# Two blocks in float32 on one core: in the last mixer the norms, the mask casts and the third output pair change place, and so does the preparation of x in the embedding before it

## The reference

```python
h = h + (p[i] @ ple_w_proj[i]) * sigmoid(rms_norm_2(h, ln_ple[i]) @ ple_w_gate[i])      # embedding
kv = rms_norm_2(h, kv_norm) @ w_kv            # k: rms_norm_2 over each head of 128, v plain
q = rms_norm_2(rms_norm_2(h, ln_mix[1]) @ w_q, q_norm) * 128 ** -0.5
# per head: A[t,s] = sigmoid(z_ts) * prod_{s<j<t} (1 - sigmoid(z_tj)), s < t;  o = A @ v
h = h + concat(o) @ w_out                     # then norm and the FFN
```

## Time and profile before

| | |
|---|---|
| median of 3 runs | 2504.65 us (2503.08 to 2505.79) |
| profiled execution | 2505.2 us |
| its span, first to last instruction | 2503.4 us |
| TensorE busy, of the span | 98% |
| VectorE, ACT, POOL busy | 68%, 50%, 54% |
| mean granted clock of TensorE | 0.996 |

### The profile page before, as it was taken

One profiled execution on the slowest core, in us unless ns is written; L12 is line 12 of the kernel. 1 busy time (PEld: TensorE's weight loads), 2 busy tenths in 40 slices (PEclk: granted clock), 3 DMA queues, 4 the chain that ended last, 5 costly groups with the idle time before them and its releaser, 6 DMA issues.

```text
span 2503.4 us, 37950 instructions
## 1 busy us (share of the span) xinstructions
PE 2456.0 (98%) x15202; PEld 2109.7 (84%) x15202; DVE 1710.7 (68%) x2551; ACT 1250.7 (50%) x1799; POOL 1358.0 (54%) x672
## 2 busy tenths in 40 slices
PE   9999999999999999999999999999999999999999
PEld 6899987777789999867878789999877777999987
DVE  6777752878587777586666677776587566777764
ACT  5434343568554333567555653333455685333343
POOL 4677744222457777346544357777444224777754
PEclk9999999999999999999999999999999999999999
DMA  4333333121323333222111123333332113233333
GB/s 142 101 102 101 102 122 107 58 68 51 91 95 102 102 102 102 85 85 85 51 35 35 51 93 102 102 102 110 94 95 83 49 34 101 102 102 101 102 104 124
DMA packets 61790, 223.64 MB, mean 89 GB/s; under 512 B 6704, under 2 KB 6832, under 8 KB 61488
## 3 DMA queue, kind: packets, MB, share of 16 engines
q1 hardware_dynamic: 60928, 218.07, 26.9%
q10 hardware_dynamic: 688, 3.15, 0.4%
HBM read 219.10 MB, written 2.10 MB: 88 GB/s over the span
## 4 chain that ended last, share of the span: by engine, by line
PE 80%; DVE 10%; ACT 6%; issue 3%; POOL 1%; DMA 1%; SPq 0%; DVEq 0%; ACTq 0%; POOLq 0%
PE ps L693 6%; PE ps L694 6%; PE ps L695 6%; PE ps L615 5%; PE ps L617 5%; PE ps L616 5%; PE ps L607 4%; PE ps L606 4%; PE ps L605 4%; PE ps L1045 2%; PE ps L1047 2%; PE ps L1046 2%; PE ps L667 2%; PE ps L1846 2%; PE ps L668 2%
## 5 line engine op out<-in xcount | busy, mean ns | idle before, releaser
L3015 POOL TENSOR_TENSOR w_lo<-raw,w_hi 128x1024 fp32r<-128x1024 f32 (+1 forms) x405 | 942.4, 2337 | 955.0 <-ACT w_hi L496 954.8
L496 ACT ACTIVATE w_hi<-raw 128x1024 fp32r<-128x1024 f32 (+1 forms) x405 | 396.8, 983 | 642.7 <-PE ps L607 392.5
L3022 POOL TENSOR_TENSOR t_lo<-t_sum,t_hi 128x1024 fp32r<-128x1024 f32 x140 | 336.2, 2423 | 60.0 <-DVE t_sum L805 36.5
L693 PE MATMUL ps<-mid_hi,w_hi 128*128 128x512 f32 x704 | 275.9, 392 | 3.4 <-DVE h L928 3.4
L694 PE MATMUL ps<-mid_lo,w_hi 128*128 128x512 f32 x704 | 275.6, 392 | 0.0
L695 PE MATMUL ps<-mid_hi,w_lo 128*128 128x512 f32 x704 | 274.8, 390 | 0.0
L615 PE MATMUL ps<-sx_hi,t_hi 128*128 128x256 f32 x840 | 238.4, 284 | 3.5 <-DVE ff_up L869 3.2
L616 PE MATMUL ps<-sx_lo,t_hi 128*128 128x256 f32 x840 | 237.7, 283 | 0.0
L617 PE MATMUL ps<-sx_hi,t_lo 128*128 128x256 f32 x840 | 237.7, 283 | 0.0
L928 DVE SCALAR_TENSOR_TENSOR h<-ps,h 128x512 f32<-128x512 f32 x320 | 200.4, 684 | 30.7 <-PE ps L695 20.5
L501 ACT ACTIVATE t_hi<-t_sum 128x1024 fp32r<-128x1024 f32 x140 | 147.3, 1060 | 103.6 <-DVE t_sum L803 65.8
(11 more groups left out here) (455 smaller groups left out, 6434.4 us busy)
## 6 DMA issues: line engine op xcount, KB each, us to landing
raw<-in_units_dram SPq DMA_DIRECT2D x406, 512.0 KB, 3.5
h<-in_x_t_dram SPq DMA_DIRECT2D x4, 512.0 KB, 7.7
toep<-in_rel_table_dram ACTq DMA_DIRECT2D x1, 2048.0 KB, 8.0
out_dram<-h SPq DMA_DIRECT2D x4, 512.0 KB, 5.5
p_f<-in_p_t_dram ACTq DMA_DIRECT2D x2, 512.0 KB, 3.7
const<-in_constants_dram SPq DMA_DIRECT2D x1, 832.0 KB, 8.2
vec<-in_vectors_dram SPq DMA_DIRECT2D x1, 137.5 KB, 2.0
```

What stands on the lines that cost most here:

```text
L496: nc.scalar.activation(w_hi[:, n % W_SLOTS, begin:], raw[:, n % RAW_SLOTS, begin:], ACT.Copy).then_inc(s_whi, 1)
L693: nc.tensor.matmul(out, hi, mid_hi[:, mid, :], start=(k == 0), stop=False)
L3015: nc.gpsimd.tensor_tensor(w_lo[:, n % W_SLOTS, begin:], raw[:, n % RAW_SLOTS, begin:], w_hi[:, n % W_SLOTS, begin:].bitcast(F32), ALU.subt ...
L3022: nc.gpsimd.tensor_tensor(t_lo[x % 2][part][:, :, :], t_sum[x % 2][part][:, :, :], t_hi[x % 2][:, 2 * part:2 * part + 2, :].bitcast(F32), ...
```

## The change

In `act_embed` and `dve_embed` the preparation of tile u-1 (its high half and square on ACT, its low half on VectorE) stands ahead of the sigmoid of step u and of the product behind it; VectorE's sum of squares stays behind the addition. In the mixer ACT's `norms` run behind that step's rounding and square. VectorE casts the masks ahead of the v columns. Half of the third pair's first unit (tiles 0 and 1, banks 1 and 2) runs after the values of head 6, half of its second unit (banks 6 and 7) between the suffixes and values of head 7, the two other halves behind the last head; both units count as used at the end. No instruction is added or removed.

```diff
@@ act_embed
                 if u:
                     act_ahead(act, n0, 0, u)
+                if gain is not None and u:
+                    act_prep(act, w, [u - 1], gain, lambda m: act.wait_ge(s_hup, w.hups + m + 1), x_hi=mid_hi)
                 act.wait_ge(s_free, b0 + u + 5)
                 nc.scalar.activation(ff_gate[:, u % 2, :], ff_gate[:, u % 2, :], ACT.Sigmoid).then_inc(s_gact, 1)
-                if gain is not None:
-                    if u:
-                        act_prep(act, w, [u - 1], gain, lambda m: act.wait_ge(s_hup, w.hups + m + 1), x_hi=mid_hi)
@@ dve_embed
                 nc.vector.tensor_tensor(ff_gate[:, u % 2, :], ps[:, 4 * g + u % 4, :], rstd[:, :], ALU.mult).then_inc(s_free, 1)
+                if gain is not None and u:
+                    dve_rest(dve, w, u - 1, gain, x_hi=mid_hi, x_lo=mid_lo)
                 dve.wait_ge(s_gact, (w.plo // 2 - 1) * 8 + u + 1)
...
                 if gain is not None and u:
-                    dve_prep(dve, w, [u - 1], gain, x_hi=mid_hi, x_lo=mid_lo)
+                    dve_square_sum(dve, w, u - 1, gain)
@@ pe_mixer3
-            def out_unit(unit, side, kp, final):
+            def out_unit(unit, side, kp, final, ms=range(4), done=1):
...
-                for m, bank in enumerate(SIDES3[side]):
+                for m in ms:
+                    bank = SIDES3[side][m]
...
-                        if m == 0:
+                        if m == ms[0]:
...
-                last.then_inc(s_used, 1)
-
-            out_unit(n_t, 0, 2, False)
-            out_unit(n_t + 1, 1, 2, False)
+                if done:
+                    last.then_inc(s_used, done)
...
             for x in range(8):
                 suffixes(x)
                 spare(STEP3[x][0])
+                if x == 7:
+                    assert next(stream, None) is None
+                    out_unit(n_t + 1, 1, 2, False, (2, 3), 0)
                 values(x)
                 spare(STEP3[x][1])
                 if x < 6:
                     scores(x + 2)
+                if x == 6:
+                    out_unit(n_t, 0, 2, False, (0, 1), 0)
                 spare(STEP3[x][2])
+            out_unit(n_t + 1, 1, 2, False, (0, 1), 0)
+            out_unit(n_t, 0, 2, False, (2, 3), 2)
             out_unit(n_t + 2, 0, 3, True)
             out_unit(n_t + 3, 1, 3, True)
@@ act_mixer3
             for u in range(16):
-                if u in (6, 10, 14):
-                    norms(u // 4 - 1)
                 if u:
                     act_ahead(act, n0, 0, u)
                     square(u - 1)
+                if u in (6, 10, 14):
+                    norms(u // 4 - 1)
@@ dve_mixer3
             layer = w.square_layer(4)
+            nc.vector.tensor_copy(tri_r[:, 0, :], mask["neg_tri"]).then_inc(s_tri, 1)
+            nc.vector.tensor_copy(tri_r[:, 1, :], mask["neg_ones"]).then_inc(s_tri, 1)
             dve.wait_ge(s_rcol, 2)
...
-            nc.vector.tensor_copy(tri_r[:, 0, :], mask["neg_tri"]).then_inc(s_tri, 1)
-            nc.vector.tensor_copy(tri_r[:, 1, :], mask["neg_ones"]).then_inc(s_tri, 1)
```

More of the change, by code:

```diff
@@ L2716, in spare @@
                     next(stream)
[L2718 to L2729, removed]
             w.unit += 8
@@ L2754, in out_unit @@
                         last.then_inc(s_bank, 1)
-                last.then_inc(s_used, 1)
-            out_unit(n_t, 0, 2, False)
-            out_unit(n_t + 1, 1, 2, False)
+                if done:
+                    last.then_inc(s_used, done)
+            for x in range(2):
+                scores(x)
+                spare(FIRST3[x])
+            for x in range(8):
+                suffixes(x)
+                spare(STEP3[x][0])
+                if x == 7:
+                    assert next(stream, None) is None
+                    out_unit(n_t + 1, 1, 2, False, (2, 3), 0)
+                values(x)
+                spare(STEP3[x][1])
+                if x < 6:
+                    scores(x + 2)
+                if x == 6:
+                    out_unit(n_t, 0, 2, False, (0, 1), 0)
+                spare(STEP3[x][2])
+            out_unit(n_t + 1, 1, 2, False, (0, 1), 0)
+            out_unit(n_t, 0, 2, False, (2, 3), 2)
             out_unit(n_t + 2, 0, 3, True)
```

## The result

The changed kernel takes 2510.95 us (median of 7 runs, 2510.27 to 2512.41), the kernel before beside it 2503.81 (2501.77 to 2505.79): ratio 1.0029, 95% interval 1.0020 to 1.0039, so slower by 5 to 10 us. The profiled execution took 2511.39 us, its span 2509.6, against 2503.4.

The account below looks back on a forecast made before the run. TensorE, busy 98% of the span, was taken to bound the kernel. Terms -2.8 - 0.9 + 0.5 + 2.3 + 2.2 + 4.4 = +5.7 us on 2505.2 gave 2510.9, or 2510.4 on the median's scale; range 2504.5 to 2515.

Parts of the forecast that it names:

- Norms, -2.8: Mixer steps 6, 10 and 14: norms behind the square spare TensorE 0.93 us three times; -2.8 us, bounds -2.8 to -2.0.
- Masks, -0.9: First head: TensorE waits for the third v column instead of the mask casts; -0.93 us, at most 1.3 gained.
- Embedding, +0.5: Embedding steps: POOL blocks VectorE's sum of squares each time, so TensorE's last k comes later; +0.5 us, bounds -1.5 to +1.5.
- Pair, +2.3: Around the last heads: the moved third pair waits 6.0 us for w_lo; net +2.3 us, bounds 2.0 and 2.8.
- Clock, +2.2: TensorE's clock falls to its lower level around the 6.0 us wait for w_lo; +2.2 us, bounds 1.7 and 3.4.
- FFN entry, +4.4: FFN's first gate unit: late roundings and blocked VectorE delay tile 7's low half; +4.4 us, bounds 2.5 and 6.
- rival 3: The clock falls once more, in the wait for x at the FFN; 1 to 2.5 us, total 2512.5; chance 0.20.
- in several pieces: Sign at the FFN's first unit: x_lo waited for by 3 us and more, split over several waits.
- Rival 1: FFN entry catches up: VectorE's first low half slips between POOL's two w_lo; x late 1 to 2, total 2507 to 2508; chance 0.21.
- Rival 2: Embedding gains what is meant: POOL falls on VectorE's gate, 1.5 us of lateness goes; total 2508.4; chance 0.10.
- Rival 4: Third pair finds its weights in time, so no long wait, low clock or late FFN entry; -6.9, 2497.7; chance 0.05.

Follow-up runs that it names:

- x first: The changed kernel with ScalarE's rounding of the third unit's weights and its successor at the FFN's entry behind preparing tiles 0 to 3: 2509.99 us, 1.0022.
- the best version: Kernel before plus norms, masks and pair moves, last-mixer weight rounding one unit earlier, FFN-entry roundings behind tiles 0 to 3; embedding as before: 2499.12 us, 0.9976.
- the rounding in head 1: The 2499.12 us kernel with ScalarE's extra weight rounding in head 1 instead of a second one in head 3: 2505.80 us, ratio 1.0002.

## Why the prediction was right, and where it was off

The forecast, 2510.4 and slower by over 0.2% most likely, came out (2510.95), and so did its main mechanism: the moved pair waits for a w_lo that ACT's order makes late, and the clock and the FFN's entry follow. That it came within 0.6 us is partly luck, as is told behind the terms. By its own steps, from the stages:

- **Norms, -2.8**: -2.8 in the run without the pair. In the changed kernel B to C is only 2.1 shorter, for a low-clock stretch (1846.2 to 1849.6) that falls into it. Ln and the next sum in its bank did not meet: no wait of L2592 is left here, not even that at the third unit, which comes right behind that stretch (0.4 without the pair).
- **Masks, -0.9**: -0.84; v in their place, as said.
- **Embedding, +0.5**: +0.55 to +0.65 without the clock. The blocked sum and the gate of step 7 are in the trace where the working put them. The sum takes 2.89, where the one behind it takes 0.69, and ends 0.55 after w_lo. The gate starts at 1840.81, which is 1841.96 on the scale of before (1.15 later), against 1842.0 by count. The exclusive lock of VectorE and GpSimd that the prediction took from the Trainium skill (SBUF — State Buffer, "Who interferes with whom") is borne out again here.

```profile
1838.00 2.89 DVE L551 TENSOR_TENSOR sum_sq<-sum_sq,sq 128x512 f32<-128x512 f32 x1
1840.81 0.68 DVE L2518 TENSOR_TENSOR ff_gate<-ps,rstd 128x512 f32<-128x512 f32 x1
...
1837.66 2.68 POOL L3021 TENSOR_TENSOR w_lo<-raw,w_hi 128x1024 fp32r<-128x1024 f32 x1 [2.84 <-ACT w_hi L496]
...
1845.21 0.50 PE L2607 MATMUL ps<-mid_hi,w_hi 128*128 128x512 f32 x1 [1.79 <-DVE mid_lo L540]
```

- **Missed, the clock at the mixer's start**: the two waits of before, 0.66 and 0.30 idle, became one of 1.79, and the clock fell behind it, worth about 0.9 (A to C lost 1.47 beside the norms' 2.8, and 0.54 in the run where the clock held). It fell in five of the six traces with the embedding's change, and in none of the seven without it. No term of the sum had it.
- **Pair, +2.3**: 2.3, once the matmuls in the wait keep the clock up. The wait is 5.92 past the pace against 6.0 by count. (The prediction's own steps, 2083.7 less 2081.3, give 2.4.)
- **Clock, +2.2**: 1.3. The low stretch began before the wait ended and covered only seven matmuls; 6.8 us of it cost 1.6 in the run with the pair alone and 1.4 in the one with x first. The mid value between two far rows was too high; the lower bound, 1.7, from the wait of the same kind, was the nearer.
- **FFN entry, +4.4**: 6.0. The count ends at the last x_lo, and that part held: it ends at 2102.99, 21.4 after the last pair's start (2081.63), against 20.9 by count and 16.5 before, so 4.9 later. The rest, about 1.1, is the clock, which fell in the wait. At half pace TensorE comes to the last tile at 2104.27, 1.3 after its x_lo was there; in the kernel before it began that tile 0.05 after. This is rival 3, to which the prediction gave 0.20 and 1 to 2.5 us. From the last pair's start to the end of the first unit it took 23.5, against 22 by count.
- **The wait there was of another kind.** The prediction had TensorE wait for x_lo "in several pieces". It waited once, ahead of the unit's first matmul, for VectorE to take h's tile 4 out of PSUM, and then found every x_lo ready when it came to it at half pace. No term or rival had this wait. The count still came near, because the same chain of VectorE makes both late. With x first on ScalarE the clock held and the pieces showed.
- **Rival 1** fell: VectorE's first low half began 0.57 behind the second w_lo, by the count's own margin. Its price was wrong too: in the run with the unused matmuls that low half did slip in first, and the stage was 1.3 longer all the same, with the next operation held by POOL instead. **Rival 2** fell in every run with the embedding's change. **Rival 4** needed a w_lo that starts before 2056.5; it started at 2058.54, which is 2061.9 on the scale of before (3.33 later at D).

The total fits better than the terms, and that is luck. The measured stages give +7.4 against +5.7: 0.9 more at the mixer's start and 1.6 more at the FFN's entry, against 0.9 less for the clock behind the pair. The time differs by 7.1, with an interval of 5 to 10; the absolute figure came nearer because the kernel before ran at 2503.81 beside the changed one and not at the 2504.65 that the forecast stood on. The high bounds of the prediction, added up as its terms give them, make +10.8 and not +12.7; its range does not hang on that.

Why the pair's move, with its weights in time, gives 1.0 and not 3.7, the best version shows: D to E is 2.6 shorter (3.7 less the 1.0 that the second rounding costs head 3), and E to F 1.6 longer, with x_lo late by 1.1 twice. No version was found in which both go, so whether they can stays open. So does why the clock held once behind the same wait of 1.8.

## What to carry to other kernels

Work moved ahead to fill a wait brings its own operands' due times with it: follow its weights back through every engine's order (here TensorE, POOL, ACT, the load's buffer) before counting the wait as filled, and move the producers in the same edit. An earlier producer has a window of its own: one step too early and it stands in its engine's queue for a buffer, with everything critical behind it. Price a new wait at least twice, once as the wait and once at the next stage, where freed buffers, loads and the first x come later too. And where the profile names no releaser, read the waits of that line in the program one by one against the times: here the wait for x_lo and the wait for a PSUM bank stand next to each other, and only the second fits.

## What the runs showed of the hardware

- The granted clock fell in or behind each wait of TensorE of 3.7 us and more in this stretch (5.8, 5.3, 4.6, 4.2, 4.0 and 3.7 idle), but for the one that was filled with unused matmuls. Near 1.7 it went either way: it fell behind the 1.8 of the embedding five times in six. Of the four traces with the 1.67 of head 7's suffixes it fell in one, with norms and masks alone (from 2058.8), and it held behind the 1.7 at the FFN's first unit in both traces that have it. In the run with the rounding in head 1 it fell once at 2096.7, with two waits of 0.9 and no longer one near; with the same two waits in the best version it held.
- Behind the same wait for w_lo the low stretch was 3.4 us long in the changed kernel and 6.8 with the pair alone and with x first; it cost the stage 1.3, 1.6 and 1.4, by the run in which the clock held. All are under half the stretch, since part of it lay in the wait. At the FFN 6.8 us cost about 1.1, since TensorE would have waited for x_lo without it.
- Taking away 1.3 us of low clock's cost gave no gain that could be measured: the next stage lost as much, with x_hi 0.5 later and another VectorE operation held by POOL.
